# Block 2 of a two-block model: one triangular inverse kept upright and turned by VectorE, output gates as seven quarter products

## The reference, cut to what matters

```
h = rmsnorm(x) * (1 + scale) + shift
p = h @ w_in                       # c_val, c_gate, c_og, ts, r_og, g_conv, g_rwkv
y_conv = conv branch(c_val, c_gate, c_og)
y_rwkv = rwkv branch(ts, r_og)     # 16 heads of 64; per step:
    sk    = state . kk_t
    state = state * w_t - sk b_t + v_t k_t
m = sigmoid(g_conv) * y_conv + sigmoid(g_rwkv) * y_rwkv
out = rmsnorm(x + gate * (m @ w_out))
```

## Time and profile before

| | |
|---|---|
| median of 3 runs | 1098.51 us (1097.63 to 1099.61) |
| the profiled execution | 1098.23 us, span 1096.4 us |
| TensorE busy | 1085.6 us, 99% |
| VectorE busy | 702.8 us, 64% |
| ScalarE, GpSimd busy | 233.1 us, 147.8 us |
| block 2's eight pairs | from 623.8 us to 994.7 us of the span |

### The profile page before, as it was taken

How to read it: one execution, slowest core, us unless ns; L and a number is a source line. 1 busy time by engine, 2 the same in 40 slices (tenths; PEclk the granted TensorE clock), 3 DMA queues, 4 the chain that set the end, 5 groups by cost and what they waited for, 6 DMA issues and landing times.

```text
span 1096.4 us, 22053 instructions
## 1 busy us (share of the span) xinstructions
PE 1085.6 (99%) x9150; PEld 929.3 (85%) x9150; DVE 702.8 (64%) x1600; ACT 233.1 (21%) x610; POOL 147.8 (13%) x204
## 2 busy tenths in 40 slices
PE   9999999999999999999999999999999999999997
PEld 8899899999988599999546888888888888887883
DVE  4376674766743477777657677666766667666465
ACT  4131221313200111010002331322223132324101
POOL 1100000000045221100330012020120202020042
PEclk9999999999999999999999999999999999999999
DMA  8677657553366446564562432333232332161251
GB/s 294 235 274 256 191 176 229 178 173 97 116 212 229 153 80 232 194 214 155 185 256 97 135 85 91 102 98 111 78 108 87 98 96 61 41 231 40 79 152 38
DMA packets 62773, 163.26 MB, mean 149 GB/s; under 512 B 8625, under 2 KB 22865, under 8 KB 62674
## 3 DMA queue, kind: packets, MB, share of 16 engines
q1 hardware_dynamic: 61666, 160.22, 45.3%
q10 hardware_dynamic: 1008, 1.63, 0.4%
HBM read 160.73 MB, written 1.11 MB: 148 GB/s over the span
## 4 chain that ended last, share of the span: by engine, by line
PE 94%; DVE 5%; DMA 1%; issue 0%; ACT 0%; POOL 0%; DVEq 0%; ACTq 0%; POOLq 0%
PE bank L813 21%; PE bank L966 20%; PE bank L465 19%; PE bank L879 6%; DVE arena L2357 3%; PE bank L1123 3%; PE bank L625 3%; PE bank L745 2%; PE bank L788 2%; PE bank L1279 2%; PE bank L1110 2%; PE bank L941 1%; PE bank L1001 1%; PE bank L541 1%; PE bank L947 1%; PE bank L979 1%
## 5 line engine op out<-in xcount | busy, mean ns | idle before, releaser
L966 PE MATMUL bank<-hT,slots 128*128 128x256 f32 x1120 | 254.6, 382 | 0.0
L966 PEld LDWEIGHTS bank<-hT,slots 128*128 128x128 f32 x1120 | 209.8, 190 | 28.4
L465 PE MATMUL bank<-hT,slots 128*128 128x256 f32 x544 | 119.7, 379 | 0.0
L465 PEld LDWEIGHTS bank<-hT,slots 128*128 128x128 f32 x544 | 103.0, 190 | 14.4 <-issue 0.6
L2357 DVE SCALAR_TENSOR_TENSOR arena<-padA,par,arena 128x256 f32<-128x256 f32 x232 | 114.1, 556 | 0.0
L465 PE MATMUL bank<-arena,slots 128*128 128x256 f32 x432 | 94.2, 379 | 0.7 <-DMA slots<-in_w_br 0.7
L465 PEld LDWEIGHTS bank<-arena,slots 128*128 128x128 f32 x432 | 81.9, 190 | 12.2 <-DMA slots<-in_w_br 1.1
L813 PE MATMUL bank<-hT,slots 128*128 128x128 f32 x736 | 91.7, 276 | 0.0
L813 PEld LDWEIGHTS bank<-hT,slots 128*128 128x128 f32 x736 | 86.7, 192 | 0.7 <-issue 0.7
L2787 POOL TENSOR_TENSOR arena<-arena 128x256 f32<-128x256 f32 x40 | 33.2, 853 | 358.7 <-PE bank L941 297.1
L813 PE MATMUL bank<-arena,slots 128*128 128x128 f32 x640 | 79.6, 275 | 0.0
(11 more groups left out here) (433 smaller groups left out, 1701.1 us busy)
## 6 DMA issues: line engine op xcount, KB each, us to landing
slots<-in_w_rwkv SPq DMA_DIRECT2D x72, 512.0 KB, 3.6
slots<-in_w_heads SPq DMA_DIRECT2D x68, 512.0 KB, 4.6
slots<-in_w_gu SPq DMA_DIRECT2D x44, 512.0 KB, 4.5
arena<-in_ada_w SPq DMA_DIRECT2D x24, 512.0 KB, 5.3
slots<-in_w_down SPq DMA_DIRECT2D x20, 512.0 KB, 4.0
slots<-in_w_br SPq DMA_DIRECT2D x32, 256.0 KB, 2.7
slots<-in_w_out SPq DMA_DIRECT2D x16, 512.0 KB, 4.2
slots<-in_w_y SPq DMA_DIRECT2D x16, 512.0 KB, 5.8
```

The lines of the kernel that those rows point to most:

```text
L465: end = e.matmul(psum, w[:, k * P:(k + 1) * P], rhs[:, k, :], start=k == 0, stop=k == kt - 1)
L966: end = e.matmul(proj(w, q), slot[w][:, k * P:(k + 1) * P], hT[:, k, :], start=k == 0, stop=k == KT - 1)
```

## The change

**Inverses.** Only `Xs` is made on TensorE: `inverted(l)` of levels 1 to 4 is one product of `Zs` by all 64 columns of `Gs` (eight matmuls 64x64 by 64x64, bank 3), and ScalarE copies the new halves from it. `Zs` is no longer multiplied but is `Xs` turned by one VectorE instruction (`turned(l)`, a transpose of 128x256 in squares of 32) that waits for ScalarE's copy. At level 0 it is the other way round: VectorE turns GpSimd's `Zs` into `Xs`, so that the product `N1` and VectorE's two steps behind it go; GpSimd makes `Zs` before its block of level 1. Level 5 stays.

**Output gates.** For pairs 0 to 6 the two gates are one product of 256 channels by 256 tokens, made from seven products of quarters (`own_gate_pair`): 28 matmuls 128x128 by 128x128 in place of 16 by 128x256. It needs sums of quarters: of `h` once (`quarter_sums`, four adds 128x512), of the weights for each pair (`slice_sum(0)` to `(3)`, four adds 128x512 on VectorE) and of the results (`first_quarter` at the end of the pair, `other_quarters`, three adds, at the start of the next). ScalarE copies one quarter (`bp1`) and applies both tanh a pair later, from SBUF. The loads of both gates' weights wait for the last of the two; three early loads of output weights wait until pair 6 is through.

```diff
@@ projections behind pair j
-                for w in OWN:
+                for w in (OGP, ROG):
                     yield from projection(e, w, j)
+                yield from own_gate_pair(e, j)
@@ inverted(l), TensorE
-                for b, lhs, rhs, half_of in ((3, Z, Gs, 0), (2, Gs, Z, 1)):
-                    if l < LEVELS - 1 or half_of:
-                        for c in range(CHUNKS):
-                            for r in HEAD_ROWS:
-                                end = e.matmul(bank[b][r, c * HD // 2:(c + 1) * HD // 2].rearrange("p (n s) -> p n s", s=size),
-                                               lhs[r, c, :], columns_of(rhs[r, c, :], half_of, size), start=True, stop=True)
+                for c in range(CHUNKS):
+                    for r in HEAD_ROWS:
+                        if l < LEVELS - 1:
+                            end = e.matmul(chunks(half(3))[r, c, :], Z[r, c, :], Gs[r, c, :], start=True, stop=True)
+                        else:
+                            end = e.matmul(bank[2][r, c * HD // 2:(c + 1) * HD // 2].rearrange("p (n s) -> p n s", s=size),
+                                           Gs[r, c, :], columns_of(Z[r, c, :], 1, size), start=True, stop=True)
@@ pe_rwkv
-                products(e, chunks(half(3)), A, B).then_inc(*pe.step(f"N1.{j}"))
@@ VectorE
+            def turned(l):
+
+                e.wait_ge(*(act.upto(f"X{l}.{j}") if l else pool.upto(f"Z0.{j}")))
+                to, of, name = (Zs[j % 2], Xs, "Z") if l else (Xs, Zs[j % 2], "X")
+                e.transpose(flat(to), flat(of)).then_inc(*dve.step(f"{name}{l}.{j}"))
```

More of the change, by code:

```diff
@@ L969, in projection, with gate_banks_of, own_gate_pair @@
                 yield
+        def gate_banks_of(q):
+            return [view3(bank[PLACE[w, q] % 2][:, :], P) for w in (GCP, GRP)]
+        def own_gate_pair(e, q):
+            one, two = gate_banks_of(q)
+            low, high = hT[:, 0:4, :], hT[:, 4:8, :]
+            first, second = (slot[w] for w in (GCP, GRP))
+            parts = ((one, 0, first[:, 0:512], low[:, :, tokens(0)]), (one, 1, first[:, 512:], high[:, :, tokens(0)]), (one, 2, bs[0], bt[1]),
+                     (two, 0, second[:, 0:512], bt[0]), (two, 1, bs[1], bt[2]), (two, 2, bs[2], high[:, :, tokens(1)]), (two, 3, second[:, 512:], bt[3]))
+            for n, (out, at, w, rhs) in enumerate(parts):
+                if n == 0:
+                    e.wait_ge(*in_slot[GCP].upto(f"rw{GCP}.{q}"))
+                    read_out(e, PLACE[GCP, q] - 2)
+                if n == 2:
+                    e.wait_ge(*dve.upto("bt4"))
+                    e.wait_ge(*dve.upto(f"bs4.{q}"))
+                if n == 3:
+                    read_out(e, PLACE[GRP, q] - 2)
+                for k in range(4):
+                    end = e.matmul(out[:, at, :], w[:, k * P:(k + 1) * P], rhs[:, k, :], start=k == 0, stop=k == 3)
+                    if k == 3 and n in (2, 6):
+                        end.then_inc(*pe.step(f"b126.{q}" if n == 2 else f"p{GRP}.{q}"))
+                    if k % 2:
+                        yield
         def layer_sum(e, w, src):
@@ L1625, in act_rwkv @@
                 e.activation(tokV[j % 2], chunks(bank[2][:, T:]), ACT.Copy).then_inc(*act.step(f"tokV.{j}"))
+            if j == 0:
+                act_gate(e, 1)
+            if levels and chain:
+                for w, to in (("gc", GC[:, p, :]), ("gr", GR[:, p, :])):
+                    e.wait_ge(*dve.upto(f"bq1221.{p}"))
+                    e.activation(to, to, ACT.Tanh, scale=0.5).then_inc(*act.step(f"{w}.{p}"))
             if more and j:
@@ L2432, in dve_rwkv @@
             if chain:
                 forced(0)
-            if levels:
-                e.wait_ge(*pe.upto(f"N1.{j}"))
-                e.tensor_tensor(Xs, chunks(half(3)), each(cst2_of("off_first")), ALU.mult).then_inc(*dve.step(f"X0.m.{j}"))
+            if levels and chain:
+                other_quarters(p)
             if chain:
@@ L2475, in dve_rwkv @@
             if levels:
-                inverted(2)
+                turned(2)
             if more:
+                slice_sum(1)
+                slice_sum(2)
                 shift(e, "k", j + 1)
@@ L2529, in dve_rwkv @@
             if levels:
-                inverted(4)
+                turned(4)
             if more:
+                slice_sum(3)
                 og_silu()
@@ L2561, in dve_rwkv @@
                 taps(e, j + 1, 13 if chain else 10, 18)
+            if more:
+                first_quarter(j)
             if end:
```

69 lines of the change are left out of this document (56 added, 13 removed).

## The result

| | before | after |
|---|---|---|
| median | 1098.88 us (1097.63 to 1099.61, 4 runs) | 1084.51 us (1084.26 to 1084.81, 4 runs) |
| span of the profiled execution | 1096.4 us | 1083.0 us |
| a middle pair, from bonus product to bonus product | 49.97 us | 48.29 us |
| pair 0, pair 1, pair 7 with what follows | 41.09, 49.53, 130.61 us | 39.51, 47.81, 128.74 us |

A middle pair is one of pairs 2 to 6; its row is their mean. The ratio is 0.9871, its 95% interval 0.9853 to 0.9888. The forecast was 1085 us, and the sum said 13.4 us less for the span; it is 13.4 less by the rounded spans, 13.5 by the traces' ends.

What follows compares the result with a forecast made beforehand. TensorE was taken as the bound, busy 1085.6 of 1096.4 us. Matmuls removed win 25.0 us, waits for VectorE lose 11.6, so 13.4 off 1098.2 gives 1084.8, forecast 1085 us; range 1076 to 1092.

Steps and rivals of the forecast that it cites:

- C: Behind level 2: the turn waits for ScalarE's copy of `Xs`, two sums follow, TensorE waits 0.95 us ahead of `solved(2)`.
- other signs: Expected in the profile after, among others: TensorE idle 0.5 to 0.7 us before `forced(1)`, a middle pair of 48.4 us.
- five of six places: Argument for the rival that no waits are paid: VectorE's slack is real in five of six places.
- The rival that no waits are paid: All 25.0 us come, 1073 us, or 1079 in a mixed case; 20% for waits not paid, wholly or half.
- A: A middle pair's start, up to `forced(1)`: taps beside GpSimd and the turn hold up the scaled state; 0.47 us lost.
- `N1`: Product of eight matmuls that goes from TensorE's list: 0.47 us won a pair.
- `inverted`, levels 1 to 4: Four levels on TensorE, 4.17 us before, 2.28 us as sixteen records of 64x64 each: 1.89 us won a pair.
- gates: Output gates on TensorE as quarter products, 6.27 us instead of 7.15: 0.88 us won in pairs 0 to 6.
- D: Behind level 4: turn and `slice_sum(3)` delay `og_silu` and `solved(3)`'s copy; 0.2 us lost before `outcome(3)`.
- the pair: Sum of the losses at A, C and D in each of pairs 2 to 6: 1.62 us.
- Pair 0: No chain, levels close together: 3.24 us won, 0.9 lost (0.5 behind level 2, 0.2 behind level 4, 0.2 at the end).
- The turn: VectorE's transpose of 128x256, not in the trace: taken as 0.42 us; forecast wrong if outside 0.3 to 0.6.

Runs made afterwards that it cites:

- inv_alone: The changed kernel with only the inverses' part, the output gates being two plain projections again; 1081.50 us, ratio 0.9844 to the kernel before.
- x2_early: The changed kernel with ScalarE's scaled state and copy of `Xs` of level 2 ahead of `act_pad` of `K_` (pairs 1 to 6); 1078.64 us.
- sums_first: The changed kernel with VectorE's two weight sums moved ahead of the turn of level 2, ScalarE's order kept; 1077.92 us.
- best_pool: best with GpSimd's blocks of levels 3 to 5 in pairs 1 to 6 moved behind `grown(2)`, as in pool_later; 1073.42 us.
- gates_alone: The changed kernel with only the output gates as quarter products, the inverses as before; 1095.22 us, ratio 0.9966 to the kernel before.
- turn_twice: The changed kernel with every turn on VectorE done twice, into the same tile; 1093.50 us, ratio 0.995 to the kernel before.
- pool_later: The changed kernel with GpSimd's blocks of levels 3 to 5 in pairs 1 to 6 made only after `grown(2)` on TensorE; 1080.90 us.
- best: The changed kernel with x2_early, sums_first, one tap moved behind the product M (pairs 1 to 6), and `rg_silu()` ahead of `inverted(5)` on VectorE; 1075.32 us.

## Why the prediction was right, and where it was not

**The mechanism at C** was right in place, cause and size: 0.95 us forecast ahead of `solved(2)`, 0.90 measured there and 1.00 with the gap behind it, six times. The idle wait of the turn was 2.78 us, not "near 2", and it changed nothing, since the end of the wait is set by ScalarE. `inv_alone`, `x2_early` and `sums_first` show the cause from three sides. Of its other signs one missed: the idle column shows 0.38 us before `forced(1)`, not 0.5 to 0.7, though from start to start it is 0.54. Its "five of six places" with slack has no count behind it: it names four, and gives three of them a loss.

**The rival that no waits are paid** would have meant 1073 us. It was wrong for the changed kernel. `best_pool`, without waits in block 2, comes to 1073.4, but by other terms: the work taken out was worth about 2.3 us less than 25.0 (below), and about as much came from A, where the kernel before waited already.

**Terms that were off**, for a middle pair:

| term | forecast | measured |
|---|---|---|
| `N1` | 0.47 | 0.47 |
| `inverted`, levels 1 to 4 | 1.89 | 4.17 - (0.61 + 0.56 + 0.61 + 0.60) = 1.79 |
| gates | 0.88 | 0.67 in the timeline, 0.65 by `gates_alone` |
| lost at A | 0.47 | 0.15 |
| lost at C | 0.95 | 1.00 |
| lost at D | 0.2 | 0.05 |
| the pair | 1.62 | 1.68 |

*The gates.* The term that was mis-sized is the quarters' time, 6.27 us forecast and 6.53 measured. The 223.5 ns of the earlier trace rows come from records that lie between 64x64 groups; the 111.9 ns of the earlier trace rows come from a stretch without any. In block 2 the quarters meet small groups at three places:

```profile
799.49 1.50 PE L1007 MATMUL bank<-hT,slots 128*128 128x128 f32 x12
800.92 0.33 PE L1111 MATMUL bank<-arena 64*64 64x64 f32 x4
...
802.95 0.71 PE L1007 MATMUL bank<-hT,slots 128*128 128x128 f32 x4
803.49 2.84 PE L1007 MATMUL bank<-slots 128*128 128x128 f32 x24
...
807.07 1.06 PE L1007 MATMUL bank<-slots 128*128 128x128 f32 x8
808.05 0.33 PE L1103 MATMUL bank<-arena 64*64 64x64 f32 x4
```

24 of them in a row take 2.68 us, 111.7 ns each as forecast. The first twelve, ahead of `solved(3)`, take 1.43 instead of 1.34; the four behind `inverted(5)` 0.54 instead of 0.45; the last eight, ahead of the next `forced(0)`, 0.98 instead of 0.90. All 56 take 1.43 + 5.10 = 6.53 us. Before, the two stretches behind level 4 held 52 records of 128x256 and took 2 x 5.81 = 11.62 us; now they hold 20 of those (4.42 us) and the quarters: 0.67 us less. The lower value that the prediction named, 0.6, came close, but not for its reason: no stall opens each of the seven groups.

*A.* From `forced(0)` to `forced(1)` TensorE took 9.43 us before and takes 9.11 after: 0.32 of `N1`'s 0.47 us arrive, where the forecast had none. The step that failed is the price of moving work within GpSimd's window. The state is scaled 8.78 us into the pair; forecast was 9.12. Two things were wrong. I charged the turn its 0.34 us in full, but a turn in the window pushes taps out of it, where they take half the time, so that it costs half; `turn_twice` shows that, where 0.48 us of turn put the scaled state 0.22 us later. That is 0.17 of the 0.34. The rest lies in the first three taps, which took 0.71 us each and not 0.83. Singly, the first took 0.40 and the other two 0.87 each; the first tap behind the turn took 0.51 and the next 0.86, and in the kernel before the first of the nine took 0.54. So by the starts the first tap of a run is the cheap one beside GpSimd, and the turn makes two runs of one; why the first is cheap is open. In return A holds more than the prediction thought: in `pool_later` `inverted(1)` starts 8.89 us into the pair, in the changed kernel 9.53, and before 9.85. So 0.64 us a pair was left there, most of it a wait that the kernel before paid too.

*D.* I had counted 0.2 us of loss; 0.05 came (from `solved(3)` to `inverted(5)` 1.49 us, before 1.44). The place and the limit were right. `og_silu` starts 1.07 us later against `solved(3)` (forecast 1.12), and the copy of `solved(3)` follows the reciprocal at once. The steps that failed are small: the copy starts 0.08 us before the reciprocal's end, so that it is 0.49 us late and not 0.64, and it takes 0.16 us and not 0.22. That uses up the cover before `outcome(3)`, and `turn_twice` shows that nothing is left of it: there `outcome(3)` comes 0.47 us later for 0.48 us of turn.

*Pair 0* won 1.58 us, not 2.34. Here the prediction missed a wait: the quarter product that writes the bank which `rg_silu` reads (L2488) waits 0.72 us.

```profile
659.90 2.05 PE L1007 MATMUL bank<-slots 128*128 128x128 f32 x16 [0.72 <-DVE arena L2488]
```

The prediction looked at what VectorE has to deliver, and not at what it has to have read before a bank is written again. `gates_alone` has the same wait, `best` with `rg_silu()` earlier has none. Pair 1 won 1.72 (1.54 forecast), pair 7 with what follows 1.87 (1.46).

*The cancelling.* Over the program the gates brought 1.5 us less than forecast (7 times 0.21), the inverses 0.8, the losses in pair 0 with its unseen wait were some 0.4 more than foreseen, C 0.3 more: about 3.0 us too much. A gave back 1.9 (six times 0.32), D some 0.7, pair 7 0.5 and the late start foreseen for pair 1 about 0.3: 3.4 us. The few tenths between the two lie in terms of some hundredths a pair and in the 0.11 us by which pair 0 starts later in the trace after, less than the traces differ there anyway.

**The turn** takes 442 ns (40 of them), 0.42 was taken. The Trainium skill's bf16 figure with the columns doubled (VectorE: DVE Perf Modes, The three transpose paths) had given an estimate of 0.44 us, and a time 0.5 us longer, which would have been the better price by 0.02 us. The prediction doesn't show how it came to it: twice the page's 311 ns would be 0.62 us, and 0.44 needs the second 128 columns at 0.13 us, which no run here shows by itself. The row:

```profile
L2476 DVE STREAM_TRANSPOSE arena<-arena 128x256 f32<-128x256 f32 x40 | 17.7, 442 | 36.2 <-ACT arena L1649 36.1
```

Behind its busy time and mean stands its idle time: 36.1 us of waiting for one line of ScalarE ahead of 17.7 us of work.

## What to carry to other kernels

When a step's producer changes from one engine to another, look at what the new producer does just before: the step inherits the waits of that whole queue, and everything behind it on its own engine does too. Then put work that needs nobody ahead of the step that waits, not behind it; here the same two sums cost 1.00 us a pair behind the turn and nothing ahead of it. And read the cost of a wait from start to start of the next product that matters: the idle column showed 0.73 us where 1.00 was lost, 0.38 where 0.64 was, and none where a tap moved away left 0.15.

## What the runs showed of the hardware

- VectorE beside GpSimd: a tap (two SBUF inputs, 128x256) takes 0.41 us alone. Of the six behind the turn, the 0.99 us after GpSimd's end hold 2.4, so the other 3.6 took 2.91 us, 0.81 each; in the middle of the run it is 0.87 from start to start. An add of 128x512 from SBUF takes 1.10 instead of 0.65 to 0.69 us, a transpose of 128x256 takes 0.43, no more than the 0.45 of the turns alone. GpSimd slows as well: a two-operand step of 128x256 takes 4.38/5 = 0.88 us beside the taps, 2.55/3 = 0.85 us beside the sums in `best_pool`, and 2.10/3 = 0.70 us in `pool_later`, where VectorE is mostly idle:

```profile
774.88 2.10 POOL L2885 TENSOR_TENSOR arena<-arena 128x256 f32<-128x256 f32 x3 [11.02 <-PE bank L1153]
```

- Sixteen records of 64x64 behind each other cost 0.47 us, but 0.56 to 0.61 from start to start ahead of a 128x128 or 128x256 group. Quarter products of 128x128 cost 0.08 to 0.09 us more where they meet such a small group (1.43, 0.54 and 0.98 us against 1.34, 0.45 and 0.90 by their mean). So at these places a change between the forms cost TensorE about 0.1 us; what causes it no run tells.
